# Streaming the tokens of the weight-stationary products from the last to the first, and reading PSUM in reverse

## The chip, the cores and the metric

The kernel runs on one NeuronCore of one Trainium2 chip. The metric is the device time of one execution in microseconds (us); the time before is the median of three runs, 3211.2 us. TensorE, VectorE, ScalarE and GpSimd stand in the profile as PE, DVE, ACT and POOL, the TensorE weight load as PEld, and the DMA queue of SyncE as SP.

## The reference

Two transformer blocks run one after the other on 256 tokens of width 2048, all in float32:

```
x1 = x  + mix1(rmsnorm(x) @ w_in) @ w_out          # two kinds of attention, 16 heads
x2 = x1 + relu(rmsnorm(x1) @ w_up)**2 @ w_down     # 2048 -> 8192 -> 2048
x2 = rmsnorm(x2)
y1 = x2 + mix2(rmsnorm(x2) @ w_in_2) @ w_out_2     # two recurrent mixers
y2 = y1 + peer(rmsnorm(y1))
out = rmsnorm(y2)
```

`peer` computes a query product (2048 by 2048) and from it scores against two sets of 128 keys, takes the best 16 of the 16384 experts for each of 8 heads, and adds `gate * gelu(u_e . x) * v_e` over the experts chosen. The kernel computes `u . x` for all 16384 experts as a dense product (2048 by 16384), multiplies by a gate that is zero where an expert was not chosen, and multiplies by all `v` (16384 by 2048).

## The kernel before

All weights stream from HBM in chunks of 128 by 2048 float32 values (1 MB) into one of four slots of `raw`. ScalarE rounds a chunk to `hi` (`make_hi`, line 262), VectorE forms the rest `lo = raw - hi` (`make_lo`, line 269), both in the reduced type fp32r. Each product of float32 operands is then three fp32r products: high with high, high with low, low with high. The activations are split in the same way into `xh` and `xl` (16 slices of 128 features by 256 tokens).

There are two ways in which a chunk is multiplied. In `multiply` (lines 272 to 283) and its relatives the activations are loaded into the array as the stationary operand, and the weights are streamed, 512 columns at a time. In `multiply_up` (lines 295 to 307) it is the other way round, and this is the function that the change touches: a 128 by 128 piece of the weights is stationary, and the 256 tokens of a feature slice are streamed as the moving operand, so that the result has output features on the partitions and tokens along the free axis. One chunk is 4 slices by 4 column blocks by 3 products, 48 matmuls of 256 columns. Four chunks make a block: 512 output features by 256 tokens, 128 partitions by 1024 float32 values, which fills one pair of PSUM banks (`pj[0]` or `pj[1]`).

`multiply_up` is called in three places, 208 chunks in all: the first product of the MLP (`mlp_pe`, 16 blocks), the query product (`query_pe`, 4 blocks) and the `u` product of `peer` (`up_block`, 32 blocks). `up_view` is the view in which a finished block is read out of its PSUM pair, 4 rows of 256 tokens. It has three readers: VectorE at line 396 (`hid = max(psum, 0) * rs_row`, 16 times), ScalarE at line 2126 (`qT = psum`, 4 times) and VectorE at line 2424 (`hidU = psum * rs_rowU`, 32 times).

Each engine has its instructions in an order written out by hand, and semaphores tie the engines together. The weights run three chunks ahead (`AHEAD = 3`): `make_hi` of a chunk waits for `pe_used`, the count of chunks that TensorE has done with, so that the slot is free; `make_lo` waits for `hi_ready`, and TensorE for `lo_ready`. A read-out waits for `pe_used` of the block's last chunk. TensorE waits for the read-out of a pair before it writes the pair again: for `m_up` before the second product of a down block in the MLP (line 342), for `wq_evac` before the scores and the third query block, for `u_left` of the block before last in `peer` (line 2293). From block 10 to block 25 of the `u` product, VectorE, ScalarE and GpSimd also build the gates: each chunk is followed on TensorE by 4 small products (line 2285), and VectorE runs lines 2400, 2405 and 2413 beside its chunk.

Of the kernel before, what the change touches and what calls it, by code (L numbers as in the profile page):

```python
# [118 lines left out]
def two_blocks(nc, x_d, xT_d, cst_d, att_d, small_d, gfin1_d, gfin2_d, wf_d, wba_d, keys_d,  # L119
# [5 lines left out]
    with ctx:  # L125
# [5 lines left out]
        def sb(name, shape, dt=F32, at=None):  # L131

            size = 4 * int(np.prod(shape[1:]))
            t = nc.alloc_sbuf_tensor_at(name, shape, dt, offset=cursor[0] if at is None else at)
            if at is None:
                cursor[0] += (size + 31) // 32 * 32
            return t
# [5 lines left out]
        hi = sb("hi", [P, SLOTS, CH], F32R)  # L143
        at_lo = cursor[0]
        lo = sb("lo", [P, SLOTS, CH], F32R)
# [15 lines left out]
        xh = sb("xh", [P, KT, TT * P], F32R)  # L161
        xl = sb("xl", [P, KT, TT * P], F32R)
# [132 lines left out]
        def multiply_up(pe, q, j, pair, k0, first, last):  # L295

            pe.wait_ge(lo_ready, q * SLOTS + j + 1)
            for k in range(4):
                end = last and k == 3
                for b in range(4):  # L300
                    cols = slice(k * NB + b * P, k * NB + b * P + P)
                    o = pair[:, b // 2, (b % 2) * 256:(b % 2) * 256 + 256]
                    clears = first and k == 0 and b % 2 == 0
                    nc.tensor.matmul(o, hi[:, j, cols], xh[:, k0 + k, :], start=clears, stop=False, skip_group_check=True)  # L304
                    nc.tensor.matmul(o, hi[:, j, cols], xl[:, k0 + k, :], start=False, stop=False, skip_group_check=True)  # L305
                    mm = nc.tensor.matmul(o, lo[:, j, cols], xh[:, k0 + k, :], start=False, stop=end and b % 2 == 1, skip_group_check=True)  # L306
            mm.then_inc(pe_used, 1)

        def up_view(pair):
            return pair[:, :, :].rearrange("p a (b n) -> p (a b) n", b=2)  # L310

        def turns(eng, n, body, start=0):

# [9 lines left out]
        def mlp_pe(pe, q0, blocks, n, step, after):  # L323
            for j in range(SLOTS):
                pe.wait_ge(tp_l, 4 * n + j + 1)
                multiply_up(pe, q0, j, pj[0], 4 * j, j == 0, j == SLOTS - 1)
                step(j)

            def part(s, par, last=False):
                first = isinstance(s, int) and s == 0  # L330
                if not last:
                    if not first:
                        pe.wait_ge(m_add, s * 4 - 1)
                    for j in range(SLOTS):
                        multiply_up(pe, s * 2 + (q0 + 1), j, pj[job(par, 0, last)], 4 * j, j == 0, j == SLOTS - 1)
                        if first and j == 0:
                            row_pe(pe, 0, rs_wide, pm)
                pe.wait_ge(m_coef_l, s + 1)
                for n in range(4):
                    w = 4 * s + n - (1 if last else 0)  # L340
                    if n == 1 and not last:
                        pe.wait_ge(m_up, s + 2)
                    elif not (first and n == 0):
                        pe.wait_ge(m_add, w if n == 0 or last else w - 1)
                    multiply(pe, s * 2 + (q0 + (1 if last else 2)), n, pj[job(par, 1 + n, last)],
                             coef_h[par], coef_l[par], 0, True, True)
                    if last:
                        after(n)
            mlp_turns(pe, blocks, part)
# [41 lines left out]
        def mlp_dve(dve, q0, blocks, step, after):  # L391
            def up(s, pair, q):
                dve.wait_ge(pe_used, q * SLOTS + SLOTS)
                if not (isinstance(s, int) and s == 0):
                    dve.wait_ge(m_coef, s)
                nc.vector.scalar_tensor_tensor(hid[:, :, :], up_view(pair), 0.0, rs_row[:, :].unsqueeze(1).broadcast_to([P, 4, TT * P]),
                                               ALU.max, ALU.mult).then_inc(m_up, 1)
# [1705 lines left out]
        def query_pe(pe, n):  # L2103
            for g in range(4):
                if g >= 2:
                    pe.wait_ge(wq_evac, g - 1)
                for j in range(SLOTS):
                    if g == 0:
                        pe.wait_ge(tp_l, 4 * n + j + 1)
                    multiply_up(pe, Q_WQ + g, j, pq_[g % 2], 4 * j, j == 0, j == SLOTS - 1)  # L2110
                    if g == 0 and j == 0:
                        lift_pe(pe, n, 3, resid, out2_second, 8)
                    if g >= 1 and j == 1:
                        scores_pe(pe, g - 1)
                    if g == 2 and j == 0:
                        row_pe(pe, 1, rs_wideU, pt)

        def router_act(act, b, j):

            if b < 0:  # L2120
                return
            if j == 0:
                act.wait_ge(pe_used, (Q_WQ + b) * SLOTS + SLOTS)
                if b >= 2:
                    act.wait_ge(r_S, b - 1)
                nc.scalar.activation(qT[b % 2][:, :, :], up_view(pq_[b % 2]), ACT.Copy).then_inc(wq_evac, 1)
            if j == 2:
                act.wait_ge(r_S, b + 1)
                act.wait_ge(nm_rs, 5)
                for t in range(TT):  # L2130
                    ins = nc.scalar.activation(sc[:, t, 4 * b:4 * b + 4, :].rearrange("p a n -> p (a n)"), pm[:, t, :], ACT.Copy,
                                               scale=stat[:, 6 + t:7 + t])
                ins.then_inc(r_sc, 1)
# [262 lines left out]
        def peer_dve(dve, n):  # L2396
# [23 lines left out]
            def scale_up(s, par):  # L2420
                dve.wait_ge(pe_used, (s + Q_PEER) * SLOTS + SLOTS)
                if not (is_block(s, 0) or is_block(s, 1)):
                    dve.wait_ge(u_out[par], (s - (2 + par)) * 8 + 16 if not isinstance(s, int) else 16 * (s // 2))
                nc.vector.tensor_tensor(hidU[par][:, :, :], up_view(pq_[par]), rs_rowU[:, :].unsqueeze(1).broadcast_to([P, 4, TT * P]),
                                        ALU.mult).then_inc(u_left, 1)
# [405 lines left out]
```

## Time and profile before

| | |
|---|---|
| median of 3 runs | 3211.2 us (3210.97 to 3211.51) |
| profiled execution, first to last instruction | 3209.0 us |
| mean granted TensorE clock | 0.999 of full speed |
| TensorE busy | 3191.6 us, 99% of the span |
| VectorE busy | 2030.1 us, 63% |
| ScalarE busy | 1447.3 us, 45% |
| GpSimd busy | 496.9 us, 15% |
| HBM traffic | 200 GB/s over the span |

The profiled execution is given by its span alone; the median of the runs is 2.2 us longer than this span. Matmuls are pipelined, so one matmul's duration in the profile is longer than the distance from its start to the start of the next; where matmuls follow each other without a break, it is this distance (the pitch) that counts, and it is read from the starts in the timeline.

### The profile page before, as it was taken

Reading aid. Unit: us, or ns where it says so; the run is one execution under the profiler, and the core shown is the slowest. Engines: PE = TensorE matmul, PEld = TensorE weight load, DVE = VectorE, ACT = ScalarE, POOL = GpSimd, SP = SyncE. Lnnn points to the kernel's source line nnn. Section 1 sums busy time; section 2 is a strip of 40 time slices with the busy share of each in tenths; the row PEclk is TensorE's granted clock in tenths of the full one; section 3 lists DMA queues with packets and bytes.
Section 4 is the critical chain, followed back from the end, with each engine's and each line's share of the span. In section 5 each row is a group of like instructions: output and inputs, shape, how many; then the busy total and the mean of one; then the engine's idle time right before and its main releaser. Section 6 shows DMA issues by size and latency. Waiting matters only on the chain.

```text
span 3209.0 us, 48201 instructions
## 1 busy us (share of the span) xinstructions
PE 3191.6 (99%) x19975; PEld 2854.0 (89%) x19975; DVE 2030.1 (63%) x1837; ACT 1447.3 (45%) x1271; POOL 496.9 (15%) x418
## 2 busy tenths in 40 slices
PE   9999999999999999999999999999999999999999
PEld 7888899999999888888989999999999888888887
DVE  5455665556555667765476888999975555555554
ACT  5454453333433364464444444555544433334333
POOL 0000000000000002136200002888840000000000
PEclk9999999999999999999999999999999999999999
DMA  7444565555555453342255566677676656556563
GB/s 282 165 159 158 172 225 194 196 186 193 195 187 193 158 183 119 132 158 105 93 211 204 199 216 222 224 251 251 229 263 259 241 225 261 228 230 257 226 261 118
DMA packets 129572, 644.18 MB, mean 201 GB/s; under 512 B 12672, under 2 KB 45840, under 8 KB 60304
## 3 DMA queue, kind: packets, MB, share of 16 engines
q1 hardware_dynamic: 95792, 623.03, 53.3%
q10 hardware_dynamic: 33632, 18.99, 1.9%
q8 instruction: 116, 1.90, 0.2%
q14 instruction: 32, 0.26, 0.0%
HBM read 606.31 MB, written 35.66 MB: 200 GB/s over the span
## 4 chain that ended last, share of the span: by engine, by line
PE 97%; DVE 1%; ACT 1%; DMA 0%; SPq 0%; issue 0%; DVEq 0%; ACTq 0%
PE pj L305 12%; PE pj L304 12%; PE pj L306 12%; PE pj L282 7%; PE pj L281 7%; PE pj L280 7%; PE pj L1774 4%; PE pj L1772 4%; PE pj L890 4%; PE pj L892 4%; PE pj L1773 4%; PE pj L891 4%; PE pm L282 2%; PE pt L282 2%; PE pt L281 2%; PE pm L281 2%
## 5 line engine op out<-in xcount | busy, mean ns | idle before, releaser
L262 ACT ACTIVATE hi<-raw 128x2048 fp32r<-128x2048 f32 x534 | 1023.8, 1917 | 1372.7 <-PE pj L306 640.7
L269 DVE TENSOR_TENSOR lo<-raw,hi 128x2048 fp32r<-128x2048 f32 x400 | 918.5, 2296 | 677.5 <-ACT hi L262 676.7
L304 PE MATMUL pj<-xh,hi 128*128 128x256 f32 x3328 | 919.9, 276 | 0.0
L305 PE MATMUL pj<-xl,hi 128*128 128x256 f32 x3328 | 918.8, 276 | 0.0
L306 PE MATMUL pj<-xh,lo 128*128 128x256 f32 x3328 | 918.8, 276 | 0.0
L305 PEld LDWEIGHTS pj<-xl,hi 128*128 128x128 f32 x3328 | 625.0, 188 | 0.6
L304 PEld LDWEIGHTS pj<-xh,hi 128*128 128x128 f32 x3328 | 624.8, 188 | 0.6
L306 PEld LDWEIGHTS pj<-xh,lo 128*128 128x128 f32 x3328 | 624.8, 188 | 0.0
L269 DVE TENSOR_TENSOR lo_in<-raw,hi 128x2048 fp32r<-128x2048 f32 x134 | 308.1, 2300 | 268.9 <-ACT hi L262 268.4
L2495 POOL TENSOR_SCALAR hotA<-cst,slotT 128x128 fp32r<-128x128 f32 x256 | 337.9, 1335 | 462.0 <-ACT slotT L2333 425.4
L1772 PE MATMUL pj<-hi,xh 128*128 128x512 f32 x576 | 232.3, 403 | 0.0
L1774 PE MATMUL pj<-hi,xl 128*128 128x512 f32 x576 | 226.6, 393 | 0.0
L1773 PE MATMUL pj<-lo_in,xh 128*128 128x512 f32 x576 | 224.9, 390 | 0.0
L282 PE MATMUL pj<-hi,coef_l 128*128 128x512 f32 x512 | 201.7, 394 | 0.0
L281 PE MATMUL pj<-lo,coef_h 128*128 128x512 f32 x512 | 200.6, 392 | 0.0
L890 PE MATMUL pj<-hi,xh 128*128 128x512 f32 x496 | 197.8, 399 | 1.2 <-DVE lo_in L269 1.2
L280 PE MATMUL pj<-hi,coef_h 128*128 128x512 f32 x512 | 198.9, 389 | 0.0
L282 PE MATMUL pj<-hi,cV_l 128*128 128x512 f32 x496 | 195.4, 394 | 0.0
L892 PE MATMUL pj<-hi,xl 128*128 128x512 f32 x496 | 194.9, 393 | 0.0
L281 PE MATMUL pj<-lo,cV_h 128*128 128x512 f32 x496 | 194.4, 392 | 0.0
L891 PE MATMUL pj<-lo_in,xh 128*128 128x512 f32 x496 | 193.3, 390 | 0.0
L280 PE MATMUL pj<-hi,cV_h 128*128 128x512 f32 x496 | 192.4, 388 | 0.0
(408 smaller groups left out, 4243.8 us busy)
## 6 DMA issues: line engine op xcount, KB each, us to landing
raw<-w_peer SPq DMA_DIRECT2D x256, 1024.0 KB, 6.3
raw<-w_mlp SPq DMA_DIRECT2D x128, 1024.0 KB, 4.8
raw<-w_in SPq DMA_DIRECT2D x102, 1024.0 KB, 4.8
raw<-w_out SPq DMA_DIRECT2D x32, 1024.0 KB, 4.8
raw<-w_q SPq DMA_DIRECT2D x16, 1024.0 KB, 4.9
act_scratch<-hidU SPq DMA_DIRECT2D x32, 512.0 KB, 3.0
gates_scratch<-stage ACTq DMA_DIRECT2D x8, 2048.0 KB, 17.5
hidV<-act_scratch SPq DMA_DIRECT2D x32, 512.0 KB, 3.7
```

What stands on the lines that cost most here:

```text
L262: nc.scalar.activation(hi[:, j, :], raw[:, j, :], ACT.Copy).then_inc(hi_ready, 1)
L269: nc.vector.tensor_tensor(low(q)[:, j, :], raw[:, j, :], hi[:, j, :].bitcast(F32), ALU.subtract).then_inc(lo_ready, 1)
L280: nc.tensor.matmul(pair[:, t, :], sh[:, k0 + k, tok], hi[:, j, cols], start=begin, stop=False)
L281: nc.tensor.matmul(pair[:, t, :], sh[:, k0 + k, tok], lo[:, j, cols], start=False, stop=False)
L282: mm = nc.tensor.matmul(pair[:, t, :], sl[:, k0 + k, tok], hi[:, j, cols], start=False, stop=end)
L304: nc.tensor.matmul(o, hi[:, j, cols], xh[:, k0 + k, :], start=clears, stop=False, skip_group_check=True)
L305: nc.tensor.matmul(o, hi[:, j, cols], xl[:, k0 + k, :], start=False, stop=False, skip_group_check=True)
L306: mm = nc.tensor.matmul(o, lo[:, j, cols], xh[:, k0 + k, :], start=False, stop=end and b % 2 == 1, skip_group_check=True)
L1772: nc.tensor.matmul(pair[:, t, :], xh[:, k0 + kk, tok], hi[:, j, cols], start=begin, stop=False)
L1773: nc.tensor.matmul(pair[:, t, :], xh[:, k0 + kk, tok], lo_in[:, j, cols], start=False, stop=False)
L1774: mm = nc.tensor.matmul(pair[:, t, :], xl[:, k0 + kk, tok], hi[:, j, cols], start=False, stop=end)
L2495: ins = nc.gpsimd.tensor_scalar(hotA[u % 2][:, a, :], cst[:, C_IOTA, :], slotT[:, 0, tok:tok + 1], None, ALU.is_equal)
```

## The change

The moving operand of all three products in `multiply_up` is the same slice of `xh` or `xl`, read with a step of -1 along the tokens. The order of the matmuls, the stationary operand and the place of the result in PSUM stay as they are, so token 255 lands in the first column of each row of 256 and token 0 in the last. `up_view`, through which all three readers read, turns each row round again, so what they write to SBUF is laid out as before.

```diff
@@ multiply_up
                     o = pair[:, b // 2, (b % 2) * 256:(b % 2) * 256 + 256]
                     clears = first and k == 0 and b % 2 == 0
-                    nc.tensor.matmul(o, hi[:, j, cols], xh[:, k0 + k, :], start=clears, stop=False, skip_group_check=True)
-                    nc.tensor.matmul(o, hi[:, j, cols], xl[:, k0 + k, :], start=False, stop=False, skip_group_check=True)
-                    mm = nc.tensor.matmul(o, lo[:, j, cols], xh[:, k0 + k, :], start=False, stop=end and b % 2 == 1, skip_group_check=True)
+                    nc.tensor.matmul(o, hi[:, j, cols], xh[:, k0 + k, :][:, ::-1], start=clears, stop=False, skip_group_check=True)
+                    nc.tensor.matmul(o, hi[:, j, cols], xl[:, k0 + k, :][:, ::-1], start=False, stop=False, skip_group_check=True)
+                    mm = nc.tensor.matmul(o, lo[:, j, cols], xh[:, k0 + k, :][:, ::-1], start=False, stop=end and b % 2 == 1, skip_group_check=True)
             mm.then_inc(pe_used, 1)
 
         def up_view(pair):
-            return pair[:, :, :].rearrange("p a (b n) -> p (a b) n", b=2)
+            return pair[:, :, :].rearrange("p a (b n) -> p (a b) n", b=2)[:, :, ::-1]
```

## Rows read from the trace of the kernel before

**Rows 1.** The page: span, busy time by engine, granted clock in 40 slices.

```profile
span 3209.0 us, 48201 instructions
...
PE 3191.6 (99%) x19975; PEld 2854.0 (89%) x19975; DVE 2030.1 (63%) x1837; ACT 1447.3 (45%) x1271; POOL 496.9 (15%) x418
...
PEclk9999999999999999999999999999999999999999
```

**Rows 2.** The page: the chain that ended last, by engine and by line.

```profile
PE 97%; DVE 1%; ACT 1%; DMA 0%; SPq 0%; issue 0%; DVEq 0%; ACTq 0%
PE pj L305 12%; PE pj L304 12%; PE pj L306 12%; PE pj L282 7%; PE pj L281 7%; PE pj L280 7%; PE pj L1774 4%; PE pj L1772 4%; PE pj L890 4%; PE pj L892 4%; PE pj L1773 4%; PE pj L891 4%; PE pm L282 2%; PE pt L282 2%; PE pt L281 2%; PE pm L281 2%
```

**Rows 3.** The page: groups of instructions; busy us, mean ns of one | idle before.

```profile
L304 PE MATMUL pj<-xh,hi 128*128 128x256 f32 x3328 | 919.9, 276 | 0.0
L305 PE MATMUL pj<-xl,hi 128*128 128x256 f32 x3328 | 918.8, 276 | 0.0
L306 PE MATMUL pj<-xh,lo 128*128 128x256 f32 x3328 | 918.8, 276 | 0.0
...
L282 PE MATMUL pj<-hi,coef_l 128*128 128x512 f32 x512 | 201.7, 394 | 0.0
...
L280 PE MATMUL pj<-hi,cV_h 128*128 128x512 f32 x496 | 192.4, 388 | 0.0
```

**Rows 4.** Timeline of TensorE, one block in the MLP; start us, duration us.

```profile
485.48 0.28 PE L304 MATMUL pj<-xh,hi 128*128 128x256 f32 x1
...
507.04 0.28 PE L305 MATMUL pj<-xl,hi 128*128 128x256 f32 x1
507.15 0.28 PE L306 MATMUL pj<-xh,lo 128*128 128x256 f32 x1
```

**Rows 5.** Timeline of TensorE: plain float32 products of an attention head, two instructions each.

```profile
85.99 0.60 PE L686 MATMUL pj<-qkT 128*128 128x256 f32 x2
86.42 0.38 PE L687 MATMUL pj<-qkT 128*128 128x128 f32 x2
```

**Rows 6.** Timeline of TensorE: the transposes at line 495, four in one row.

```profile
411.16 0.60 PE L495 MATMUL pm<-cst,resid 128*128 128x128 f32 x4
```

**Rows 7.** Line 495: ns min/median/max, first and last start us.

```profile
L495 PE MATMUL pm<-cst,resid x48: 270/272/273, 411.2 to 1682.4; 128*128 128x128 f32 x48
```

**Rows 8.** Groups of VectorE by form: the read-outs, and two reductions over 1024 values.

```profile
L2424 DVE TENSOR_TENSOR hidU<-pj,rs_rowU 128x1024 f32<-128x1024 f32 x32 | 38.9, 1215 | 0.0
L1239 DVE TENSOR_REDUCE haT<-hA 128x128 f32<-128x1024 f32 x16 | 32.2, 2015 | 0.5
L396 DVE SCALAR_TENSOR_TENSOR hid<-pj,rs_row 128x1024 f32<-128x1024 f32 x16 | 19.6, 1225 | 18.3 <-PE pj L306 18.3
...
L1712 DVE TENSOR_REDUCE mss<-dsq 128x8 f32<-128x1024 f32 x2 | 2.4, 1220 | 0.1
```

**Rows 9.** Groups of ScalarE by form: copies out of PSUM.

```profile
L2340 ACT ACTIVATE stage<-pm 128x512 f32<-128x512 f32 x32 | 36.1, 1128 | 0.0
...
L1169 ACT ACTIVATE hqk<-pm 128x512 f32<-128x512 f32 x8 | 4.8, 599 | 21.2 <-PE pm L1130 21.2
...
L2126 ACT ACTIVATE qT<-pj 128x1024 f32<-128x1024 f32 x4 | 4.0, 1006 | 0.0
```

**Rows 10.** Timeline of TensorE in the MLP: a block's end, the next two products' first matmuls.

```profile
463.39 0.28 PE L306 MATMUL pj<-xh,lo 128*128 128x256 f32 x1
463.50 0.39 PE L280 MATMUL pj<-hi,coef_h 128*128 128x512 f32 x1
...
469.00 0.39 PE L280 MATMUL pj<-hi,coef_h 128*128 128x512 f32 x1
```

**Rows 11.** Timeline of VectorE at the same place; in brackets idle before and its releaser.

```profile
463.71 1.23 DVE L396 SCALAR_TENSOR_TENSOR hid<-pj,rs_row 128x1024 f32<-128x1024 f32 x1 [1.14 <-PE pj L306]
465.71 2.29 DVE L269 TENSOR_TENSOR lo<-raw,hi 128x2048 fp32r<-128x2048 f32 x1 [0.78 <-ACT hi L262]
```

**Rows 12.** Timeline of ScalarE in the query product.

```profile
1699.14 1.92 ACT L262 ACTIVATE hi<-raw 128x2048 fp32r<-128x2048 f32 x1 [0.88 <-PE pj L306]
1700.96 1.00 ACT L2126 ACTIVATE qT<-pj 128x1024 f32<-128x1024 f32 x1
```

**Rows 13.** Line 2099, the scores: ns min/median/max, first and last start us.

```profile
L2099 PE MATMUL pm<-keys,qT x64: 270/275/275, 1709.8 to 1782.6; 128*128 128x128 f32 x64
```

**Rows 14.** Timeline of VectorE in the first blocks of peer's u product.

```profile
1798.00 1.22 DVE L2424 TENSOR_TENSOR hidU<-pj,rs_rowU 128x1024 f32<-128x1024 f32 x1
...
1817.55 2.29 DVE L269 TENSOR_TENSOR lo<-raw,hi 128x2048 fp32r<-128x2048 f32 x1 [1.51 <-ACT hi L262]
1819.76 1.22 DVE L2424 TENSOR_TENSOR hidU<-pj,rs_rowU 128x1024 f32<-128x1024 f32 x1
```

**Rows 15.** Busy time by window (PE, PEld, DVE, ACT, POOL; clock, DMA share, GB/s): two blocks with gates.

```profile
2064.80:2088.50 23.70, 23.70 (x212) 23.70 (x211) 22.38 (x19) 12.68 (x9) 21.59 (x18) 1.00 0.55 200
2088.50:2112.00 23.50, 23.50 (x210) 23.50 (x209) 22.39 (x19) 12.70 (x9) 21.01 (x16) 1.00 0.87 291
```

## The prediction

> **What bounds the kernel now.** I read the page first: TensorE is busy for 3191.6 of 3209.0 us, and its granted clock stands in the top tenth in every slice, so there is no idle time and no clock to win back [rows 1]. Then the chain that ended last: 97% of it is TensorE, and the three lines that the change edits, 304 to 306, are the largest part, 12% each, 36% together, about 1,155 us [rows 2]. The groups by line say the same: 3 times 3328 = 9,984 matmuls of 256 columns, with no idle time before them [rows 3]. The mean of 276 ns there is not what one costs, since matmuls overlap. For that I took the timeline of one whole block: the first starts at 485.48, the 192nd at 507.15 us, 21.67 us for 191 steps, a pitch of 113.5 ns [rows 4]. By it the 9,984 take 1,133 us, which fits the 36% of the chain. The reader is to see that these matmuls follow each other with nothing between, so any change of their pitch arrives whole at the end: 1 ns more or less per matmul is 10 us.
>
> **The change, part by part.** No instruction is added, removed or moved, no DMA, no wait and no semaphore. Two access patterns get a step of -1. So there are two prices to find: the pitch of the 9,984 matmuls, and the duration of the 52 read-outs.
>
> *The stream.* No matmul of this kernel reads its moving operand with any step but +1, so the trace doesn't show the operation, and I bound it.
>
> From above: the nearest row in which TensorE streams 256 float32 columns more slowly, at the same clock, is the plain float32 product of an attention head. Its two instructions of 256 columns start at 85.99, and the next line starts at 86.42 us: 215 ns each, against 113.5 [rows 4, 5]. That is almost half the rate. If a descending fp32r stream went at it, each matmul would cost 101.5 ns more: 9,984 times 101.5 = 1,013 us.
>
> From below: could it be faster? 256 columns in 113.5 ns leave little. The four transposes at line 495 take 0.60 us from the start of the first to the end of the last; one lasts 0.27, so their pitch is (0.60 - 0.27) / 3 = 110 ns [rows 6, 7]. These are float32 instructions of 128 columns which, going by the plain products above, stream at half the column rate, so 110 ns is the same streaming time as 256 fp32r columns without the last 3 or 4 ns. If reversing the order took these away, for instance because stationary and moving reads then met less often, it would win 9,984 times 3.5 = 35 us.
>
> A small toll also has a row. Lines 280 and 282 have one shape and differ only in which tiles they read: 388 and 394 ns for 512 columns [rows 3]. So which addresses are read moves a matmul by up to 6 ns per 512 columns, 3 ns per 256: 9,984 times 3 = 30 us more.
>
> I take 0. The same bytes are read, from the same 1,024-byte stretch per partition, each word beside the one before it; only the sign of the step differs. Whatever fetches words together can still do so, as long as it doesn't demand that the lower address comes first. The row of the plain products is slower for a reason that lies in their type (one product is two instructions at half the rate), not in the order of their addresses, so as a row for this step it is far off; the fp32r rows, at 113.5 ns, are nearer.
>
> A rule speaks against this choice. The plain products show that TensorE has a rate of 215 ns for 256 columns beside that of 113.5 [rows 4, 5]. The Trainium skill, "Vector Engine (DVE) Microarchitecture Reference", section 5.2, says that a VectorE port streams at full rate only while consecutive elements come in runs of at least two adjacent 4-byte words that start on an 8-byte boundary, and gives 1.30 ns against 1.054 per column for pairs that start on an odd word. A descending stream starts on word 255, an odd one. If that held for TensorE's moving port with this ratio, the pitch would be 140 ns, and an estimate of the sum by the page is 264 us more, a time of 3475 us; by the trace's nearest rows it is 0. The page is about another engine, and no run here shows it for TensorE.
>
> *The read-outs.* Line 2424 takes 1215, line 396 1225 and line 2126 1006 ns [rows 8, 9]. No instruction reads with a negative step, so again bounds. Nothing suggests a gain: the contiguous reduction over 1024 values at line 1712 takes 1220 ns, the same as these read-outs, so they already go at the rate of a contiguous read. Above, line 1239 reduces 1024 values as well, but reads them across a row of 128, one word at a time from places 128 words apart, and takes 2015 ns: 0.8 us more [rows 8]. On ScalarE the copy at line 2340, which writes in steps of 32 words, takes 1128 against 599 ns for the plain copy at line 1169, 0.53 us per 512 values, 1.06 for the 1024 of line 2126 [rows 9]. A reversed read stays among neighbouring words, so it is nearer to the contiguous rows, and I take 0 for the durations. All exposed, the upper ends would be 48 times 0.8 plus 4 times 1.06 = 43 us. But work hides them, place by place:
>
> In the MLP a block ends, and the down product begins at 463.50. Its second quarter, which needs the pair back, begins at 469.00 [rows 10]. The read-out runs from 463.71 to 464.94, 4.06 us before that, and VectorE then idles 0.78 us before its next `lo` [rows 11]. What waits next behind it is `lo` of a chunk that TensorE reaches three chunks later. So 0.8 us more is free there.
>
> In the query product, the read-out ends at 1701.96, and the first scores that need it start at 1709.8 us [rows 12, 13]: 7.8 us of cover against 1.06.
>
> In peer, read-outs come every 21.76 us (1798.00 to 1819.76), one block of 192 matmuls [rows 14]. The `lo` before the read-out at 1819.76 was released by a `hi` that takes 1.92 us, itself released by TensorE's last chunk of the block, so the block ended near 1815.6 and the read-out is done about 5.4 us later. TensorE needs the pair one block after that end, so some 16 us are left. The tightest place is the 16 blocks with gates, where VectorE is busy for 22.38 of 23.70 and 22.39 of 23.50 us: 1.1 to 1.3 us idle per block [rows 15]. 0.8 us more fits, narrowly. If it didn't, behind the read-out there wait lines 2413, 2400 and 2405, and TensorE for the gate products: up to 16 times 0.8 = 13 us.
>
> *The sum.* 0 for the stream, 0 for the read-outs: the profiled execution would again span 3209.0 us, and the runs lie 2.2 us above it, at 3211.2.
>
> **The rivals.**
>
> *Half rate.* A descending run is not fetched as pairs: each word is a read of its own. The place is every matmul of lines 304 to 306, the price lies between 0 and the 1,013 us of the plain products' rate, and the time at that end is 4224 us. It decides as soon as the pitch passes 113.5 ns by more than a few per cent, because nothing hides it. For it speaks that 256 fp32r columns in 113.5 ns are twice the column rate of the plain products, so something in the fast path may depend on order. Against it, that the words stay neighbours. The rule of section 5.2 above is a milder form of this, and its own figure lies inside this bound. On the other hand the Trainium skill, "Advanced Engine Details and Errata", section VectorE Performance Modes, allows VectorE's packed mode a unit step of +1 or -1; no run here shows it. I give this case 0.20.
>
> *A small toll on the stream*, up to 3 ns per matmul, 3212 to 3241 us, as different addresses meet: 0.07.
>
> *The read-out shows.* If the PSUM read in reverse is slow and the cover in the gate blocks fails, up to 13 us there (3224); if it failed everywhere, 43 us, 3254 us. Against it stand the covers above. 0.07.
>
> *Faster*, the 35 us of the transposes' pitch, 3176 us: 0.06. For it there is only that 3.5 ns exist; nothing says that order causes them.
>
> That the change does nothing at all can't be told from my forecast by the time, but by the trace: the operands would be the same.
>
> **How the numbers follow.** No change, within 0.2% (6.4 us, about what a measurement of this kernel can tell from no change): 0.60, with a range of its own from 3205 to 3217. Predicted time 3211 us. The cases above it hold 0.34, below it 0.06. The range reaches down to the faster case and up to the read-out's end, 3176 to 3254, and so holds the forecast, the gain, the small toll and the read-outs, 0.80 in all; the half-rate case, 0.20, is left out, far above.
>
> **What would show it.** The step of the stream is right if the timeline again has 192 matmuls of lines 304 to 306 in 21.7 us, and the groups show 276 ns; half rate would show as about 380 ns in these groups, which is what one plain 256-column product takes (0.60 us for two less the 0.215 between them) [rows 5], and blocks of some 41 us. The read-outs are right if lines 396, 2424 and 2126 stay within 2% of 1225, 1215 and 1006 ns; if they take 2 us, the windows of the gate blocks tell whether it was covered. I would be wrong above all if TensorE's fetch of two fp32r words needs an ascending address.

## The result and the profile after

The changed kernel takes 3255.7 us (median of 4 runs, 3255.4 to 3255.8) against 3211.2, a ratio of 1.0139 with a 95% interval of 1.0124 to 1.0153: 44.5 us slower. The forecast was no change, 3211 us, and the range ended at 3254.

The page of the changed kernel, beside [rows 1]: the span is 44.7 us longer (3209.0 before), the number of instructions and the clock are the same, and TensorE is as full as before.

```profile
span 3253.7 us, 48201 instructions
...
PE 3235.9 (99%) x19975; PEld 2897.9 (89%) x19975; DVE 2027.4 (62%) x1837; ACT 1445.6 (44%) x1271; POOL 489.5 (15%) x418
...
PEclk9999999999999999999999999999999999999999
```

So the time is not idle time; TensorE itself is longer at work. Its groups on the same page, beside [rows 3], show at which instructions:

```profile
L304 PE MATMUL pj<-xh,hi 128*128 128x256 f32 x3328 | 939.0, 282 | 0.0
L306 PE MATMUL pj<-xh,lo 128*128 128x256 f32 x3328 | 936.4, 281 | 0.0
L305 PE MATMUL pj<-xl,hi 128*128 128x256 f32 x3328 | 931.0, 280 | 0.0
...
L281 PE MATMUL pj<-lo,coef_h 128*128 128x512 f32 x512 | 201.7, 394 | 0.0
L280 PE MATMUL pj<-hi,coef_h 128*128 128x512 f32 x512 | 200.9, 392 | 0.0
...
L282 PE MATMUL pj<-hi,coef_l 128*128 128x512 f32 x512 | 198.9, 388 | 0.0
```

The reader is to see two things. The three edited lines went from 276 ns to between 280 and 282 ns. And the three lines of the untouched 512-column products have exchanged their durations: line 282 had 394 and has 388, line 281 now has 394. Their sum is what it was, to within a nanosecond.

The timeline of the same block of the MLP as in [rows 4] gives the pitch: 22.50 us for 191 steps, 117.8 ns, where it was 113.5.

```profile
487.00 0.28 PE L304 MATMUL pj<-xh,hi 128*128 128x256 f32 x1
...
509.38 0.28 PE L305 MATMUL pj<-xl,hi 128*128 128x256 f32 x1
509.50 0.28 PE L306 MATMUL pj<-xh,lo 128*128 128x256 f32 x1
```

4.3 ns times 9,984 matmuls is 43 us, all but 2 us of the difference.

One stretch did not become slower, and it matters for what follows. These are the first chunk of the MLP (its 48 matmuls end at about 424 us), the eight small transposes behind it, and the stretch after them, first in the kernel before, then in the changed one:

```profile
418.65 0.28 PE L306 MATMUL pj<-xh,lo 128*128 128x256 f32 x1
...
423.95 0.28 PE L306 MATMUL pj<-xh,lo 128*128 128x256 f32 x1
424.07 1.04 PE L495 MATMUL pm<-cst,resid 128*128 128x128 f32 x8
...
425.53 0.28 PE L306 MATMUL pj<-xh,lo 128*128 128x256 f32 x1
...
446.61 0.28 PE L306 MATMUL pj<-xh,lo 128*128 128x256 f32 x1
```

```profile
418.70 0.28 PE L306 MATMUL pj<-xh,lo 128*128 128x256 f32 x1
...
424.00 0.28 PE L306 MATMUL pj<-xh,lo 128*128 128x256 f32 x1
424.12 1.04 PE L495 MATMUL pm<-cst,resid 128*128 128x128 f32 x8
...
425.58 0.28 PE L306 MATMUL pj<-xh,lo 128*128 128x256 f32 x1
...
447.49 0.28 PE L306 MATMUL pj<-xh,lo 128*128 128x256 f32 x1
```

In both kernels the 45 steps between the first two lines take 5.30 us, 117.8 ns each. Behind the transposes the 186 steps of the ascending streams take 21.08 us, 113.3 ns, those of the reversed streams 21.91 us, 117.8 ns. So 117.8 ns is a pitch that the kernel before already had, in its first chunk here and in the first chunk of the query product. The operands there are no special ones: the block of [rows 4] begins with the same tokens and the same slots of weights, at 113.5 ns.

The read-outs answer to [rows 8] and [rows 9], by form (VectorE, then ScalarE): they did not move by more than 3 ns.

```profile
L2424 DVE TENSOR_TENSOR hidU<-pj,rs_rowU 128x1024 f32<-128x1024 f32 x32 | 39.0, 1218 | 0.0
L396 DVE SCALAR_TENSOR_TENSOR hid<-pj,rs_row 128x1024 f32<-128x1024 f32 x16 | 19.6, 1225 | 21.6 <-PE pj L306 21.5
```

```profile
L2126 ACT ACTIVATE qT<-pj 128x1024 f32<-128x1024 f32 x4 | 4.0, 1007 | 0.0
```

### The profile page after: what moved, and what is told of

The parts are those of the page before. It is cut to its first block, busy times and chain, and to the rows that moved or that the text cites. A ratio compares the mean times of both kernels' runs of the same rounds, so it can differ in the third digit from the quotient of the medians.

```text
span 3253.7 us, 48201 instructions
## 1 busy us (share of the span) xinstructions
PE 3235.9 (99%) x19975; PEld 2897.9 (89%) x19975; DVE 2027.4 (62%) x1837; ACT 1445.6 (44%) x1271; POOL 489.5 (15%) x418
## 4 chain that ended last, share of the span: by engine, by line
PE 97%; DVE 1%; ACT 1%; DMA 0%; SPq 0%; issue 0%; DVEq 0%; ACTq 0%
PE pj L304 12%; PE pj L306 12%; PE pj L305 12%; PE pj L281 7%; PE pj L280 7%; PE pj L282 7%; PE pj L1774 4%; PE pj L1772 4%; PE pj L890 4%; PE pj L892 4%; PE pj L1773 3%; PE pj L891 3%; PE pm L281 2%; PE pt L281 2%; PE pt L280 2%; PE pm L280 2%
## 5 line engine op out<-in xcount | busy, mean ns | idle before, releaser
L304 PE MATMUL pj<-xh,hi 128*128 128x256 f32 x3328 | 939.0, 282 | 0.0
L306 PE MATMUL pj<-xh,lo 128*128 128x256 f32 x3328 | 936.4, 281 | 0.0
L305 PE MATMUL pj<-xl,hi 128*128 128x256 f32 x3328 | 931.0, 280 | 0.0
L2495 POOL TENSOR_SCALAR hotA<-cst,slotT 128x128 fp32r<-128x128 f32 x256 | 330.7, 1307 | 494.0 <-ACT slotT L2333 436.8
```

The costliest lines, as they stand in the source:

```text
L304: nc.tensor.matmul(o, hi[:, j, cols], xh[:, k0 + k, :][:, ::-1], start=clears, stop=False, skip_group_check=True)
L305: nc.tensor.matmul(o, hi[:, j, cols], xl[:, k0 + k, :][:, ::-1], start=False, stop=False, skip_group_check=True)
L306: mm = nc.tensor.matmul(o, lo[:, j, cols], xh[:, k0 + k, :][:, ::-1], start=False, stop=end and b % 2 == 1, skip_group_check=True)
L2495: ins = nc.gpsimd.tensor_scalar(hotA[u % 2][:, a, :], cst[:, C_IOTA, :], slotT[:, 0, tok:tok + 1], None, ALU.is_equal)
```

## The experiments

All are edits of the kernel before, unless said otherwise. "Pitch" is the distance from one start to the next in the timeline of a block, as above. Where the edit puts results in other places, the later stages compute with them, in the same time. A time without an interval is that of a single run; repeats of one kernel lay within 1.7 us of each other.

**Which half of the change costs the time.** The first has the stream reversed and the old read-out, the second the reverse.

```diff
# stream alone: multiply_up as in the change, up_view as before
# read-out alone: multiply_up as before, and
-            return pair[:, :, :].rearrange("p a (b n) -> p (a b) n", b=2)
+            return pair[:, :, :].rearrange("p a (b n) -> p (a b) n", b=2)[:, :, ::-1]
```

> Only the stream is reversed; the finished blocks are read out of PSUM as before, so their tokens land in reverse order in hid, qT and hidU and the later stages compute with permuted tokens. If the stream pays (theory stream: 4.3 ns more per matmul in the timeline of the changed kernel, times 9984 = 43 us): 3254 to 3257 us, pitch 117.8 ns. If the reversed read-outs pay (theory read-out): 3210 to 3213 us.

> Only the read-outs are reversed; the stream ascends, so again later stages compute with permuted tokens. Theory stream: 3210 to 3213 us, lines 396, 2424 and 2126 at 1225, 1215 and 1006 ns. Theory read-out: 3254 to 3257 us. If each part has its own share of the 44.5 us, both this run and the stream alone lie between.

Measured: the stream alone 3255.0 us, ratio 1.0137 (1.0120 to 1.0153); the read-out alone 3210.7 us, ratio 0.9998 (0.9989 to 1.0008). The whole 44 us belong to the stream, and a PSUM read in reverse costs nothing here, in its duration either (by form, the run with the read-out alone):

```profile
L2424 DVE TENSOR_TENSOR hidU<-pj,rs_rowU 128x1024 f32<-128x1024 f32 x32 | 38.9, 1216 | 0.0
L396 DVE SCALAR_TENSOR_TENSOR hid<-pj,rs_row 128x1024 f32<-128x1024 f32 x16 | 19.6, 1225 | 18.3 <-PE pj L306 18.3
```

**Which order costs time.** One theory is that each word below the one before it costs, another that the direction of the stream as a whole does. The 256 words are taken in groups of `w`; either the words inside a group are reversed, or the groups. The result `o` is viewed in the same groups.

```diff
-                    nc.tensor.matmul(o, hi[:, j, cols], xh[:, k0 + k, :], ...
+  words in fours:     xh[:, k0 + k, :].rearrange("p (g w) -> p g w", w=4)[:, :, ::-1]
+  groups reversed:    xh[:, k0 + k, :].rearrange("p (g w) -> p g w", w=w)[:, ::-1, :]      # w = 4, 8, 16, 64
+  halves interleaved: xh[:, k0 + k, :].rearrange("p (h g w) -> p g h w", h=2, w=4)
```

> The 256 words are streamed in groups of four (16 bytes) whose order ascends, the four words inside a group descending; read out as before, so tokens are permuted within fours. Theory word order (the port pays when a word lies below the one before it): 192 of 256 steps go down, about 0.75 of the toll or all of it: 3243 to 3256 us. [...]

> The groups of four descend, the words inside a group ascend; read out as before, so tokens are permuted. Theory word order: 63 of 256 steps go down, a quarter of the toll or none: 3211 to 3223 us. Theory direction of the whole stream: the whole toll, 3250 to 3258 us. If both this run and the one with words descending in fours are far above 3256 us, two-level patterns cost by themselves.

> The stream takes 16-byte lines alternately from the lower and the upper half of the 256 words, both ascending; no line follows the one before it in address. Read out as before, so tokens are permuted. Theory next line (the moving port pays for a line that is not the next higher one): 3254 us or more. [...]

> Four runs of 64 words, the runs in descending order, each ascending; tokens permuted. Theory next line: 3 hops down instead of 63, so 3211 to 3214 us. [...] A fixed toll for a stream that starts above its end: 3254 to 3257 us.

> Runs of 8 words (32 bytes, two lines), the runs descending, each ascending; tokens permuted. With runs of 4 the toll was whole (4.3 ns per matmul), with runs of 64 none. Theory toll per hop down (one for each step to a line that is not the next higher one, 31 instead of 63): half, 3231 to 3235 us. Theory row (lines are fetched in rows wider than a line, and going down inside a row costs): all or nothing, 3254 to 3257 if the row is wider than 32 bytes, 3209 to 3213 if it is not.

> Runs of 16 words (64 bytes), descending, each ascending; tokens permuted. Theory toll per hop: 15 of 63, 3220 to 3223 us. Theory row: 3254 to 3257 if the row is wider than 64 bytes, 3209 to 3213 if it is not.

Measured, with the pitch from the blocks of the MLP:

| stream | time us | pitch ns |
|---|---|---|
| ascending (before) | 3211.2 | 113.5 |
| words reversed inside fours | 3210.8 | 113.5 |
| groups of 64 reversed | 3210.5 | 113.5 |
| groups of 16 reversed | 3256.0 | 117.8 |
| groups of 4 reversed | 3255.9 | 117.8 |
| all reversed (the change) | 3255.7 | 117.8 |
| groups of 8 reversed | 3277.6 | 120.0 |
| halves interleaved | 3345.1 | 126.6 |

A word that lies below the one before it costs nothing here: with words reversed inside fours the pitch is that of before. So the half-rate rival falls. With it falls the use that the prediction made of the Trainium skill, "Vector Engine (DVE) Microarchitecture Reference", section 5.2, where a descending stream was to pay because it starts on an odd word: inside these fours the first word is odd as well, and nothing is paid. The rule itself is not tested, since two words read downwards still fill one 8-byte unit. But the theory of a toll per hop to a lower line falls as well. 63 hops (groups of 4) and 15 hops (groups of 16) cost the same, and 31 hops (groups of 8) cost more than either. Nor is it all or nothing by the width of a row. Several pitches appear again and again, and little between them.

**Is it the walk of the weight load?** "Two reads meeting" is the idea that the weight load and the stream hold each other up, by the way in which their reads walk. Here the stationary operand reads one word 128 times, so its load does not walk; the stream ascends, then descends.

```diff
-                    nc.tensor.matmul(o, hi[:, j, cols], xh[:, k0 + k, :], ...
+                    nc.tensor.matmul(o, hi[:, j, k * NB + b * P:k * NB + b * P + 1].broadcast_to([P, P]), xh[:, k0 + k, :], ...
```

> The stationary operand reads one word of a weight row 128 times instead of 128 different ones, so its results are not the products of the reference; the stream ascends as before. Control for the next one. Theory two reads meeting: 113.4 ns or less per matmul, 3160 to 3212 us, as the weight load no longer walks through addresses. Theory next line: 3209 to 3213 us.

> One-word weights with the stream descending (read out as before). Theory two reads meeting: the same time as with the one-word weights and the ascending stream, within 3 us, since there is no direction of the weight read left. Theory next line, or a fixed toll of the descending stream by itself: 43 us more than with the one-word weights and the ascending stream.

Measured: 3220.5 us ascending and 3254.9 descending; the difference of 34 us is neither none nor the 43 us expected. The descending stream has 117.8 ns whether the weight load walks or not, so the direction of the load's walk isn't the cause. The ascending run is the more telling one, by its timeline. These are two blocks of its MLP, the same lines with the same operands in SBUF:

```profile
486.45 0.28 PE L304 MATMUL pj<-xh,hi 128*128 128x256 f32 x1
...
508.74 0.28 PE L306 MATMUL pj<-xh,lo 128*128 128x256 f32 x1
...
530.84 0.28 PE L304 MATMUL pj<-xh,hi 128*128 128x256 f32 x1
...
552.49 0.28 PE L306 MATMUL pj<-xh,lo 128*128 128x256 f32 x1
```

The first takes 22.29 us for 191 steps, 116.7 ns, the second 21.65 us, 113.4 ns. The same instructions have more than one steady pitch.

**Does each descending stream pay for itself, and by its length?** One product of the three reversed; and, in `multiply`, the 512 weight columns reversed instead of the tokens (the sums then fall on other tokens or features).

```diff
# only line 305
-                    nc.tensor.matmul(o, hi[:, j, cols], xl[:, k0 + k, :], start=False, ...
+                    nc.tensor.matmul(o, hi[:, j, cols], xl[:, k0 + k, :][:, ::-1], start=False, ...
# 512 columns: lines 280 to 282
-                    nc.tensor.matmul(pair[:, t, :], sh[:, k0 + k, tok], hi[:, j, cols], ...
+                    nc.tensor.matmul(pair[:, t, :], sh[:, k0 + k, tok], hi[:, j, cols][:, ::-1], ...
```

> Only the second of the three products (high weights by the low part of the activations, line 305) streams in reverse, so its sums fall on the wrong tokens. Theory toll of each descending stream by itself: a third, 3225 to 3227 us. Theory carried state (one descending stream leaves the array's weight loading and streaming out of step, so that ascending streams after it pay too, as line 2285 seems to, whose ascending streams went from 113.3 to 116.9 ns in the changed kernel): more than a third, up to 3256 us.

> The token products ascend as before; the 512 columns of the weights in the function multiply are streamed in reverse (about 4,600 matmuls in the MLP's and peer's second products), so the output features land reversed in their block of 512. Toll per column or per line: twice 4.3 ns, 8.6 by 4,600: 40 us, 3249 to 3253 us. Fixed toll per matmul: 20 us, 3229 to 3233 us. No toll for this operand: 3209 to 3213.

Measured: with one product of three reversed 3260.7 us, more than with all three, and all three lines at 117.8 ns on average. And the 512-column products of the MLP, untouched, were caught too (those of `peer` kept their 228.9 ns). In the timeline of this run the first down product of the MLP has the pitch of before, the next one not:

```profile
464.16 0.39 PE L280 MATMUL pj<-hi,coef_h 128*128 128x512 f32 x1
...
485.90 0.39 PE L282 MATMUL pj<-hi,coef_l 128*128 128x512 f32 x1
...
508.74 0.40 PE L280 MATMUL pj<-hi,coef_h 128*128 128x512 f32 x1
...
530.91 0.39 PE L282 MATMUL pj<-hi,coef_l 128*128 128x512 f32 x1
```

95 steps in 21.74 us, 228.8 ns, and then 95 steps in 22.17 us, 233.4 ns, for the same ascending streams. The run with the 512 columns reversed took 3230.8 us: 4,560 matmuls (1520 of each of the three lines) at 233.3 instead of 228.9 ns. That is again 4.4 ns per matmul, the same for 512 columns as for 256, so this step goes by the matmul and not by the bytes.

**Reversal or place?** Nothing reversed; padding moves operands of TensorE against each other. Both paddings below move the tokens by 64 bytes against the weights. Then two reversed streams with the tokens moved.

```diff
# tokens moved (xh, xl 64 bytes up; what lies behind them 128 up)
+        cursor[0] += 64
         at_x = cursor[0]
         xh = sb("xh", [P, KT, TT * P], F32R)
         xl = sb("xl", [P, KT, TT * P], F32R)
+        cursor[0] += 64
# weights moved (hi, lo 64 up; what lies behind them 128 up)
+        cursor[0] += 64
         hi = sb("hi", [P, SLOTS, CH], F32R)
         at_lo = cursor[0]
         lo = sb("lo", [P, SLOTS, CH], F32R)
+        cursor[0] += 64
```

> The kernel before with xh and xl 64 bytes higher (64 bytes of padding before and after them), streams ascending: they now start on a multiple of 128 bytes, before and in the other ascending runs without a toll 64 bytes past one. Theory start address (what costs is where the first word of a stream lies, not that addresses go down): the toll without any reversal, 3250 to 3258 us. Theory descent (a stream pays when its 16-byte lines come in falling order): 3209 to 3213 us.

> Runs of 16 words in descending order with xh and xl 64 bytes higher, so that each stream starts 64 bytes past a multiple of 128, as before the change; tokens permuted. Theory start address: no toll, 3209 to 3213 us. Theory descent: 3254 to 3258 us, as without the move.

> The changed kernel with xh and xl 64 bytes higher. Theory start address: its first word is now 60 bytes past a multiple of 64 at another place in the 128 bytes, so the time may change by some us to tens of us either way, 3209 to 3290 us. Theory descent: 3254 to 3258 us, the changed kernel's own time.

> The kernel before with hi and lo 64 bytes higher and all behind lo 128 bytes higher; nothing reversed. As moving operands (7,900 matmuls of 512 columns) hi and lo now start 64 bytes past a multiple of 128, as the token streams do. Theory start address: the 512-column matmuls lose up to 4.4 ns each, the step that separated them from their descending form, 3170 to 3205 us, faster than both kernels. Theory descent: 3209 to 3213 us.

Measured: tokens moved 3293.0 us, weights moved 3266.5 us (ratio 1.0173, 1.0156 to 1.0190), both without any reversal and both with 120.0 ns for the ascending token streams. The groups of the page for weights moved (lines are 2 further on than before):

```profile
L306 PE MATMUL pj<-xh,hi 128*128 128x256 f32 x3328 | 942.6, 283 | 0.0
...
L282 PE MATMUL pj<-hi,coef_h 128*128 128x512 f32 x512 | 199.5, 390 | 0.0
L283 PE MATMUL pj<-lo,coef_h 128*128 128x512 f32 x512 | 199.4, 389 | 0.0
L284 PE MATMUL pj<-hi,coef_l 128*128 128x512 f32 x512 | 199.2, 389 | 0.0
```

So moving 64 bytes costs more than reversing. With the tokens moved, the reversed kernel takes 3277.3 us, 16 us less than the ascending one: there reversal is a gain. Groups of 16 with the old start address kept their 117.8 ns (3271.3 us, the rest from the 512-column products, 233.3 ns in that run). The theory that the stream's own start address decides falls with that, and with the weights moved, where the tokens' start address modulo 128 is unchanged.

**Own place or relative place.** The last two: all operands moved together, and the coefficients alone.

```diff
# all moved
+        cursor[0] += 64
         at_raw = cursor[0]
# coefficients moved: hid, coef_h, coef_l, ... 64 up
         xl = sb("xl", [P, KT, TT * P], F32R)
+        cursor[0] += 64
```

> The kernel before with 64 bytes of padding behind xl; nothing reversed, xh, xl, hi and lo stay. The coefficients (stationary) now lie 256 instead of 192 bytes from the weights (moving) modulo 512, as in the run with hi and lo moved, where the 512-column matmuls of the function multiply took 226.8 ns instead of 228.9. Theory relative place (the pitch depends on where the stationary operand lies against the moving one): about 4,560 times 2.1 ns less, 3200 to 3203 us, and 113.4 ns for the token streams. If the gain of that run came from the place of hi itself: 3209 to 3213 us.

> The kernel before with 64 bytes of padding ahead of the first buffer, so that all operands of TensorE move by 64 bytes together; nothing reversed. Theory relative place: nothing changes, 3209 to 3213 us, 113.4 and 228.9 ns. Theory own place (each operand has good and bad start addresses for itself, tokens 64 bytes past a multiple of 128 and weights on it): both leave their good place, 3255 us or more.

Measured: all moved 3211.2 us, and its groups repeat those of before to the digit (lines 1 further on):

```profile
L305 PE MATMUL pj<-xh,hi 128*128 128x256 f32 x3328 | 919.9, 276 | 0.0
L306 PE MATMUL pj<-xl,hi 128*128 128x256 f32 x3328 | 918.8, 276 | 0.0
L307 PE MATMUL pj<-xh,lo 128*128 128x256 f32 x3328 | 918.8, 276 | 0.0
...
L283 PE MATMUL pj<-hi,coef_l 128*128 128x512 f32 x512 | 201.7, 394 | 0.0
L282 PE MATMUL pj<-lo,coef_h 128*128 128x512 f32 x512 | 200.6, 392 | 0.0
L281 PE MATMUL pj<-hi,coef_h 128*128 128x512 f32 x512 | 198.9, 389 | 0.0
```

A common shift changes nothing, a shift of one operand against another does: relative place it is. The 512-column products in `multiply` bear it out over the kernel before and six runs. With coefficients and weights as far apart as before, their mean pitch is 228.9 ns (before, and all moved). With 64 bytes more between them it is 226.8 and 226.7 (weights moved, coefficients moved). With 128 bytes more it is 233.3 (the three runs with the tokens moved, since the coefficients lie behind the tokens).

The coefficients moved gave half of what was expected. The 512-column products took 226.7 ns as forecast, 10 us less. But the kernel took 3243.4 us (ratio 1.0102, 1.0085 to 1.0119), since the token streams, whose operands had not moved at all, went to 117.5 ns on average. The timeline of this run shows where they changed (lines 1 further on):

```profile
425.62 0.37 PE L305 MATMUL pj<-xh,hi 128*128 128x256 f32 x1
...
447.36 0.28 PE L307 MATMUL pj<-xh,lo 128*128 128x256 f32 x1
447.48 0.60 PE L443 MATMUL pm<-cst,rs_wide 128*128 128x128 f32 x4
447.84 0.36 PE L305 MATMUL pj<-xh,hi 128*128 128x256 f32 x1
448.04 0.28 PE L306 MATMUL pj<-xl,hi 128*128 128x256 f32 x1
...
464.77 0.28 PE L307 MATMUL pj<-xh,lo 128*128 128x256 f32 x1
```

Up to 447.36 us, 191 steps take 21.74 us, 113.8 ns. Then come four small instructions, which turn `rs_wide` round, and behind them the same streams take 16.73 us for 142 steps, 117.8 ns, and stay there to the end of the MLP. In the query product and at the start of `peer` they change back and forth: 239 matmuls from 1692 us on, 47 from 1738 and 191 from 1770 run at 113.4 to 113.6 ns, those around them at 117.8. No operand of theirs lies elsewhere than before; of the small instructions ahead of them `rs_wide` does, by 64 bytes. So the pitch also hangs on what TensorE did before.

## Why the prediction was wrong

*The frame held.* TensorE bounds the kernel without a gap, nothing hides a longer pitch, and no wait or engine took part: VectorE had the same durations, and its idle time in front of line 396 only grew with the blocks (18.3 to 21.6 us). *The read-outs* were priced right, at 0.

*The step that failed is "I take 0" for the stream.* It measured 4.3 ns per matmul, 43 us. The argument was about a single fetch (the same words side by side, only the sign of the step), and as far as it goes it is borne out: words falling inside fours are free, and runs of 64 words in falling order too. So the sign by which the prediction would have been wrong above all, a fetch of two words that needs an ascending address, is not what happened. Nor was it the half-rate case: its price, from 0 to 1,013 us, takes in 43, but its mechanism, each word a read of its own, does not fit words that fall inside fours for nothing. What the argument left out is that the stream doesn't run alone, and that the same ascending stream has more than one pitch. The trace of before showed that: 117.8 ns in the first chunk of the MLP, 113.3 behind it. The prediction took its pitch from one later block [rows 4] and held it for the only one. The case nearest to the truth, the small toll, was priced with a row that doesn't say what I read from it. The 388 and 394 ns of lines 280 and 282 [rows 3] were taken for the effect of the addresses that each reads. In the changed kernel the same lines, with the same addresses, have 392 and 388, and line 281 has the 394: it is one pattern over three matmuls, which can begin at any of them. So its bound of 3 ns, 30 us, had no ground, and the true 4.3 ns lay above it. The transposes [rows 6] bounded a gain that never came.

*What takes its place.* Shown: the reversed streams run at 117.8 instead of 113.4 ns, 4.4 ns more per matmul, and reversing 512 columns costs the same 4.4 ns; a step of 6.5 ns, to 120.0, comes with no reversal when the streamed operand lies 64 bytes elsewhere against the stationary one, and is gone when both move together; reversed order is slower in the old layout (113.5 to 117.8 ns) and faster in another (120 to 118.3); and the same instructions on the same operands run at 113.4 or at 117 to 118 ns, by what went before. So the runs show no price of falling addresses by themselves. They fit a picture in which the pair of reads, stationary and moving, has several steady patterns: the old layout and order fell into the fastest that was seen for the token streams after the first chunk, and the reversed streams stay in the next. That picture is inferred from the pitches, not shown.

*Open.* By which resource the two reads hold each other up was not shown. The moves also shifted the operands against what the other engines and the DMAs touch, but what these are doing at the time does not set the pitch: in the changed kernel and in the runs with tokens or weights moved, the mean pitch of the token streams is the same to within 0.2 ns whether VectorE, ScalarE, GpSimd or a DMA is at work or not. It was not shown why one reversed stream of three keeps all three in the slower pattern, or how long a pattern lasts once entered. The idea that the two reads meet more often when both walk the same way, which I held after the groups of 4, fell with the one-word weights; in which order the load reads its words, no run shows.

## What to carry to other kernels

Where TensorE streams without a gap and each matmul loads new weights, the pitch can hang, as here, on the pair of operands and on what ran before: a pad of 64 bytes or another walk through a tile can be worth several per cent of it (113.5, 117.8 and 120.0 ns here), so read the pitch from the timeline after every change of layout or order, in more than one stretch, also at lines that the change didn't touch. Two rows of one shape that differ by a few ns need not differ because of their operands; look at whether the difference stays with the line in a second trace before it is used as a price. And a PSUM read in reverse order was free on VectorE and ScalarE.

## What the runs showed that I had not expected

The pitches that returned most often fall on a grid: over three matmuls 340, 353, 360 and 380 ns for 256 columns and 680, 687 and 700 ns for 512, that is 51, 53, 54, 57, 102, 103 and 105 times 6.67 ns. Others don't (116.7 and 118.3 ns for one matmul). The cause wasn't tried.

In the timeline of the changed kernel each matmul begins together with the load of the weights for the next (start us, duration us):

```profile
488.18 0.28 PE L305 MATMUL pj<-xl,hi 128*128 128x256 f32 x1
488.19 0.19 PEld L306 LDWEIGHTS pj<-xh,lo 128*128 128x128 f32 x1
488.30 0.28 PE L306 MATMUL pj<-xh,lo 128*128 128x256 f32 x1
488.30 0.19 PEld L304 LDWEIGHTS pj<-xh,hi 128*128 128x128 f32 x1
```

So the load and the stream overlap from the start. The Trainium skill, "TensorE: Matmul & The Clock Gate", section "Back-to-back issue gap", says that the spacing in such a stream is set by the load and the matmul together. The runs agree: 64 bytes more between the two operands took it from 113.4 to 120.0 ns. The Trainium skill, "SBUF — State Buffer", section "SBUF: two separate sides", gives TensorE a second, independent read port for the loads. The runs speak against reading this as two reads that never touch each other's time: with 64 bytes more between weights and tokens the same streams took 6.5 ns more, at the same granted clock of 0.999.
